# Gated scan of the second block: gate bias fetched a stage earlier, squares of the queries and keys on ScalarE, and another order of the steps' rows

## What is computed

```python
def _mlstm_scan(q, k, v, li, lf, state):      # chunks of 128 tokens
    def step(carry, inp):
        C, n, m = carry
        qc, kc, vc, lic, lfc = inp
        b = jnp.cumsum(lfc, axis=-1)
        logd = jnp.where(mask, b[..., :, None] - b[..., None, :] + lic[..., None, :], -jnp.inf)
        inter = b + m[..., None]
        m_s = jnp.maximum(inter, jnp.max(logd, axis=-1))
        dmat = jnp.exp(logd - m_s[..., None])
        s = jnp.einsum('bhsd,bhrd->bhsr', qc, kc) * dmat
        ...
        log_w = b[..., -1:] - b + lic
        m_new = jnp.maximum(b[..., -1] + m, jnp.max(log_w, axis=-1))
        w = jnp.exp(log_w - m_new[..., None])
        decay = jnp.exp(b[..., -1] + m - m_new)
        C_new = decay[..., None, None] * C + jnp.einsum('bhr,bhrv,bhrk->bhvk', w, vc, kc)
...
gates = z[..., 4 * M_W:G_END] + b_gates       # input and forget gates; lf = log_sigmoid(forget gate)
q_a = _rms_norm(z[..., a0:a0 + A_W].reshape(B_, L_, A_HEADS, A_DH), qn_w)
k_a = _rms_norm(z[..., a0 + A_W:a0 + A_W + A_KVW].reshape(B_, L_, A_KV, A_DH), kn_w)
```

## Time and profile before

| | us |
|---|---|
| median of 3 runs | 4027.12 |
| lowest, highest | 4027.06, 4028.39 |
| profiled execution, its own time | 4033.01 |
| profiled execution, span | 4031.2 |
| TensorE busy | 3406.1 (84%) |
| VectorE busy | 1940.7 (48%) |
| ScalarE busy | 677.4 (17%) |
| GpSimd busy | 941.4 (23%) |

### The profile page before, as it was taken

One profiled execution on the slowest core, in us unless ns is written; L12 is line 12 of the kernel. 1 busy time (PEld: TensorE's weight loads), 2 busy tenths in 40 slices (PEclk: granted clock), 3 DMA queues, 4 the chain that ended last, 5 costly groups with the idle time before them and its releaser, 6 DMA issues. The chain is left out here.

```text
span 4031.2 us, 37513 instructions
## 1 busy us (share of the span) xinstructions
PE 3406.1 (84%) x11902; PEld 1511.2 (37%) x11903; DVE 1940.7 (48%) x3995; ACT 677.4 (17%) x1600; POOL 941.4 (23%) x811
## 2 busy tenths in 40 slices
PE   7988999668899987999868967789878888788877
PEld 3345444422233322333225445444333333333332
DVE  5834222522233322333225236476666766677676
ACT  1011211000000000000002125312222222222221
POOL 2000000022122222021221040014444444444443
PEclk8999999789999999999989988789999899899998
DMA  9825423369998998296975100239999999999997
GB/s 332 281 105 177 168 101 133 125 242 408 371 384 346 365 407 347 96 389 262 383 305 183 53 7 1 84 125 408 421 421 409 421 410 412 421 405 421 416 421 317
DMA packets 194149, 1157.36 MB, mean 287 GB/s; under 512 B 25659, under 2 KB 27995, under 8 KB 74356
## 3 DMA queue, kind: packets, MB, share of 16 engines
q1 hardware_dynamic: 97140, 565.17, 36.2%
q0 software_dynamic: 80576, 564.05, 34.1%
q10 hardware_dynamic: 16320, 26.75, 2.1%
HBM read 1128.96 MB, written 48.68 MB: 292 GB/s over the span
## 5 line engine op out<-in xcount | busy, mean ns | idle before, releaser
L1149 PE MATMUL ps<-wt,e_xT 128*64 128x512 f32 x3200 | 741.1, 608 | 115.5 <-DMA wt<-in_w_exp 114.7
L2559 DVE SCALAR_TENSOR_TENSOR mod<-q_uv,mix 128x1024 f32<-128x1024 f32 x512 | 627.1, 1225 | 389.7 <-DMA q_uv<-in_peer_uv,q_picks 384.4
L2264 POOL DMA_INDIRECT q_uv<-in_peer_uv,q_picks x512 | 573.5, 1120 | 997.4 <-PE ps L2356 715.8
L2356 PE MATMUL ps<-q_uv,q_dg 128*128 128x512 f32 x1024 | 517.3, 662 | 136.8 <-ACT q_dg L2433 136.7
L2356 PE MATMUL ps<-q_uv,tri 128*128 128x512 f32 x1024 | 474.7, 618 | 80.8 <-ACT tri L2433 80.4
L1129 POOL COPY wt<-e_land 128x2048 f32<-128x2048 f32 x124 | 247.9, 2029 | 1002.7 <-PE ps L1149 951.1
L1149 PEld LDWEIGHTS ps<-wt,e_xT 128*64 128x64 f32 x3200 | 219.5, 139 | 595.5 <-issue 381.6
L2356 PEld LDWEIGHTS ps<-q_uv,q_dg 128*128 128x128 f32 x1024 | 212.2, 212 | 432.9 <-issue 432.9
L1149 PE MATMUL ps<-wt,e_aT 128*64 128x512 f32 x1600 | 354.8, 596 | 2.8 <-ACT e_aT L1202 2.8
L2356 PEld LDWEIGHTS ps<-q_uv,tri 128*128 128x128 f32 x1024 | 198.5, 198 | 353.4 <-issue 353.4
L454 PE MATMUL ps<-hT,wt 128*128 128x512 f32 x640 | 285.1, 602 | 1.5 <-DVE wt L781 1.5
(11 more groups left out here) (447 smaller groups left out, 3411.8 us busy)
## 6 DMA issues: line engine op xcount, KB each, us to landing
wt<-in_w_exp SPq DMA_DIRECT2D x260, 1024.0 KB, 19.3
e_land<-in_w_exp SPq DMA_DIRECT2D x124, 1024.0 KB, 24.1
wt<-in_w_in_units SPq DMA_DIRECT2D x15, 2048.0 KB, 11.3
mod<-in_w_mod_units SPq DMA_DIRECT2D x48, 512.0 KB, 5.6
scratch_xs<-const_zeros SPq DMA_DIRECT2D x8, 2080.0 KB
mod<-in_w_ada_units SPq DMA_DIRECT2D x32, 512.0 KB, 8.5
p_ring<-in_w_in SPq DMA_DIRECT2D x7, 2048.0 KB, 10.4
e_xg<-scratch_xs ACTq DMA_DIRECT2D x104, 128.0 KB, 6.9
```

The costliest lines, as they stand in the source:

```text
L1149: ins = nc.tensor.matmul(ps[64 * h:64 * h + 64, at, :], lhs[:, k % 4, 64 * (k // 4):64 * (k // 4) + 64], wt[:, u, a, h * W:(h + 1) * W], s ...
L2264: pool.indirect_dma_start(out=uv[:, n % NR, :, :].rearrange("p a d -> p (a d)"), out_offset=None, in_=A["peer_uv"], in_offset=bass.Indirec ...
L2356: last = nc.tensor.matmul(acc(t)[:, c, :], dg(n), uv[:, n % NR, 1, c * W:(c + 1) * W], start=fresh, stop=closing)
L2559: dve.scalar_tensor_tensor(junk[:, n % 2, :], uv[:, n % NR, 0, :], 1.0, mix[:, tile_of(k), :], ALU.mult, ALU.mult, accum_out=ap[:, k % 2, ...
```

## The change

There are three edits. The bias `bg` becomes a tensor that both stages share, and SyncE fetches it in `second_project`, behind the weights; that stage ends only when it has landed. The squares are made by ScalarE behind its Ln, no longer by GpSimd, and VectorE sums them behind `aa` instead of ahead of it. And TensorE's list has the rows of steps 0 to 3 ahead of `states(0)`, and those of steps 4 and 5 ahead of the wait for the state; VectorE's `state(1)` moves from the end of step 4 to behind the six steps.

```diff
@@ build: tensors of the second block
-                     zr=sb("zr", [P, NT + NTC, 784], c=second))
+                     zr=sb("zr", [P, NT + NTC, 784], c=second),
+                     bg=sb("bg", [P, 16], c=second))
@@ second_project, SyncE, behind the last weights(n)
+                sp.dma_start(S["bg"][:, :], A["b_gates_2"].unsqueeze(0).broadcast_to([P, 16])).then_inc(s_bg, 16)
                 sp.wait_ge(s_g2, 16)
+                sp.wait_ge(s_bg, 16)
@@ second_heads
-        bg = sb("bg", [P, 16])
+        bg = S["bg"]
@@ SyncE
-                sp.dma_start(bg[:, :], A["b_gates_2"].unsqueeze(0).broadcast_to([P, 16])).then_inc(s_bg, 16)
                 sp.dma_start(negm[:, :, :], K["negm"]).then_inc(s_load, 16)
@@ GpSimd
-                pool.tensor_tensor(sq[:, :, :], zr[:, :, 16:16 + 10 * DH], zr[:, :, 16:16 + 10 * DH], ALU.mult).then_inc(s_sq, 1)
                 pool.wait_ge(s_load, 16 * 5)
                 pool.wait_ge(s_rr, 1)
@@ TensorE
                 pe.wait_ge(s_aa, 1)
-                spreads(0)
-                spreads(1)
-                spreads(2)
+                for i in range(4):
+                    spreads(i)
                 states(0)
-                spreads(3)
+                spreads(4)
+                spreads(5)
                 pe.wait_ge(s_C, 1)
                 states(1)
-                spreads(4)
-                spreads(5)
                 pe.wait_ge(s_ar, NSTEP)
@@ ScalarE, behind Ln
+                act.activation(sq[:, :, :], zr[:, :, 16:16 + 10 * DH], ACT.Square).then_inc(s_sq, 1)
                 act.wait_ge(s_rq, 1)
                 act.activation(rq[:, :, :], rq[:, :, :], ACT.Sqrt).then_inc(s_sd, 1)
@@ VectorE
-                dve.wait_ge(s_bg, 16)
                 link(dve.tensor_tensor(gt[:, :, :], zr[:, :, 0:16], bg[:, :].unsqueeze(1).broadcast_to([P, NA, 16]), ALU.add))
@@
                 dve.tensor_tensor(lf[:, :, :, :], le[:, :, :, :], lf[:, :, :, :], ALU.subtract).then_inc(s_lf, 1)
-                dve.wait_ge(s_sq, 1)
-                link(dve.tensor_reduce(rq[:, :, :].rearrange("p t h -> p (t h)"),
-                                       sq[:, :, :].rearrange("p t (h c) -> p (t h) c", c=DH), AX_X, ALU.add))
-                dve.tensor_scalar(rq[:, :, :], rq[:, :, :], 1.0 / DH, RMS_EPS, ALU.mult, ALU.add).then_inc(s_rq, 1)
                 link(dve.memset(mr[:, 0, :], 0.0))
                 dve.wait_ge(s_cum, 1)
@@
                 last.then_inc(s_aa, 1)
                 dve.wait_ge(s_aa, 1)
+                dve.wait_ge(s_sq, 1)
+                link(dve.tensor_reduce(rq[:, :, :].rearrange("p t h -> p (t h)"),
+                                       sq[:, :, :].rearrange("p t (h c) -> p (t h) c", c=DH), AX_X, ALU.add))
+                dve.tensor_scalar(rq[:, :, :], rq[:, :, :], 1.0 / DH, RMS_EPS, ALU.mult, ALU.add).then_inc(s_rq, 1)
@@
                     if i == 3:
                         state(0)
-                    if i == 4:
-                        dve.wait_ge(s_xk, 1)
-                        state(1)
@@
                 dve.tensor_scalar(eq[:, 1], eq[:, 1], -1.0, None, ALU.mult).then_inc(s_eq, 1)
+                dve.wait_ge(s_xk, 1)
+                state(1)
                 dve.wait_ge(s_xq, 1)
```

More of the change, by code:

```diff
@@ L1347, in second_project @@
         s_h, s_ht, s_hT, s_full, s_free = sem("h"), sem("ht"), sem("hT"), sem("full"), sem("free")
+        s_bg = sem("bg")
         s_dve, s_zp, s_conv, s_ct, s_kt, s_kc = sem("dve"), sem("zp"), sem("conv"), sem("ct"), sem("kt"), sem("kc")
@@ L1656, in second_heads @@
         rd = sb("rd", [P, 2, AKV])
-        s_bg, s_load, s_dve, s_abs, s_lf1, s_one, s_lf2, s_lf = (sem(n) for n in ("bg", "load", "dve", "abs", "lf1", "one", "lf2", "lf"))
+        s_load, s_dve, s_abs, s_lf1, s_one, s_lf2, s_lf = (sem(n) for n in ("load", "dve", "abs", "lf1", "one", "lf2", "lf"))
         s_cum, s_aa, s_ab, s_ar, s_ek, s_xk, s_eq, s_xq, s_wsc = (sem(n) for n in (
```

## The result

| | before | changed |
|---|---|---|
| median, us | 4027.06 (5 runs) | 4002.71 (5 runs) |
| lowest to highest | 4017.74 to 4028.39 | 3992.35 to 4007.77 |
| span of the profiled execution | 4031.2 | 3990.6 |

The ratio is 0.9943, 95% interval 0.9925 to 0.9962: 23 us faster, between 15 and 30. A later set of runs of the same two kernels gave 0.9956 (0.9942 to 0.9969; medians 4023.37 and 4005.02). The forecast was 4005.8, 21.3 less than before.

The account below looks back on a forecast made before the run. second_heads up to the end of its scan was taken to bound, its saving moving the last stage forward whole. Start 8.7 plus steps 12.7 gave 21.3 us off: 4027.1 to 4005.8, range 4002 to 4012, chance 0.72.

Parts of the forecast that it names:

- Start: Beginning of second_heads up to step 0's reduction of the running maxima on VectorE, claimed to come 8.7 us earlier.
- Steps: Six steps of running maxima on VectorE: idle times of 3.80 and 6.81 and state(1)'s 2.07 go, 12.7 us.
- No idle time is left on VectorE: In the six steps: TensorE's reordered rows arrive in time, so VectorE no longer waits for them.
- the later overlap: GpSimd's query and key chain beside VectorE's scan: shared port costs single short VectorE operations some tenths each.
- `state(1)` behind the steps: Update moved behind step 5: hidden by decayed(0)'s wait for ScalarE, so no cost taken; 2.1 us without that cover.
- the 0.9 put down for half speed: First product with CT behind the steps: possible 0.9 us cost with TensorE at half speed, not taken into the sum.
- from E to the end the same length as before: From the first instruction behind step 5 to the end of second_heads: length unchanged, no gain.
- GpSimd's chain: Queries and keys on GpSimd in second_heads: ends 17 us before TensorE wants it, instead of 29.
- rivals, 1 and 2: At second_heads' start: gate sum slow by itself, 4009.2, chance 0.05; extra table load before Square, 4007.1, chance 0.1.
- Rival 3: TensorE stays at half clock in the six steps: 15.5 us off, 4011.6, chance 0.08.
- Rival 4: Half clock over the states' rounds behind the steps makes the kernel slower, up to 8 us, 4035; chance 0.02.
- Rival 5: GpSimd's chain or the wait for the squares replaces the removed idle time: no change, 4027, chance 0.03.

Follow-up runs that it names:

- e1_bias: Kernel before with the bias alone fetched in second_project; from ScalarE's first table load in second_heads to step 0's reduction 19.37 us, before 19.62.
- e2_squares: Kernel before with squares on ScalarE and their reduction behind aa, nothing else; from ScalarE's first table load to step 0's reduction 12.92 us, before 19.62.
- e7_reduce_first: Changed kernel with the reduction of the squares put back ahead of the copies of TensorE's sums; stage start to step 0's reduction 16.42 us, changed kernel 10.78.
- e4_memset: Kernel before with GpSimd's squares replaced by a memset of the same tile; stage start to step 0's reduction 15.87 us, before 19.62.
- e3_order: Kernel before with only the order of TensorE's rows and the place of state(1) changed; whole time ratio 0.9972 (0.9961 to 0.9984).
- e11_delay: Changed kernel with two unused ScalarE copies ahead of the attention's first scores; TensorE's first query transpose to stage end 142.1 us, changed kernel 137.6 and 137.3.
- e9_early: Changed kernel with the gates' whole chain and the squares with their sums moved into second_project; 4004.65 us (0.9948 of the kernel before).
- e12_early_fill: e9_early with unused TensorE products ahead of each attention pair's scores, 22 for pairs 3 to 11, else 6; 4015.54 us (0.9976 of the kernel before).
- e13_less_fill: e12_early_fill with fewer unused products, 10 for pairs 3 to 11, else 2; 3996.88 us against 4023.44 for the kernel before (0.9935).

## Why the prediction was right

The direction, the size and the chain of reasons held. Term by term:

- **Start, 8.7 forecast, 8.84 measured.** The transfer's 2.7 and the hold of 3.85 go, and ScalarE's table becomes the next late thing, as worked out (Exp at S + 1.29). Gate sum 0.26 (0.25 forecast), Square 3.39 (3.45), reduction beside the rows of step 0. e1_bias and e2_squares show that neither of the first two gives this alone, and e7_reduce_first that the move of the reduction carries 5.6 of it. That GpSimd's instruction was the holder is shown by e4_memset, and by e1_bias, where the hold passed to the next instructions.
- **Steps, 12.7 forecast, 11.0 measured** (E - T 34.04 before, 23.03 after). Two terms of the sum were mis-sized. "No idle time is left on VectorE" was off by 0.85: TensorE's granted clock stayed at half (1.2 GHz) for longer behind the start of the rows than in the profile before, so the rows of step 1 came late. It was 0.50 to 0.52 in their first 6 us, against 0.53 in the first 4 and 1.00 after (windows below). And in step 4 VectorE's addition (L2012) was held 1.04 by GpSimd's operation of 1.26 (L1724), which starts 0.07 ahead of it and ends with it: the later overlap that I had put at some tenths.
- **`state(1)` behind the steps, nothing forecast.** The update ends at E + 3.79 and the first product with `CT` at E + 5.9, and ScalarE takes it at E + 6.59 without having waited for it (line below), so it cost nothing. E to Q is 43.99 against 44.86, and that 0.87 less need not be the change's: e4_memset, with the order of before, has 43.7, and the last product of the rounds (L1801) ran in 2.06 instead of 3.35. Also the 0.9 put down for half speed did not come: in e3_order and e7_reduce_first the product with `CT` took 3.8, and E to Q was 43.8 and 43.6.
- **Attention, nothing forecast, 2.6 to 3.2 gained.** It is the one part that I did not see, against "from E to the end the same length as before" (181.6 instead of 185.1, 3.5 less). S to Q fell by 20.7 only, and this gain made 23.4 of it for the stage. What sets this length stays open: the experiments rule out the attention's code, its start alone and its mean clock, and e11_delay shows that a delay ahead of it moves it.
- **The range.** 4002.71 lies 0.7 above its lower bound, and there luck has a part. The range gave 1.3 to the scatter of whole times, by three runs; the five runs of each kernel span 10.7 and 15.4 us, and the interval of the ratio stands for 15 to 30 us. What the runs bear out is the working inside the stage; the whole time alone could not have told 21.3 from 24.
- GpSimd's chain ended at S + 62.8, 15 us ahead of TensorE's wait (17 forecast).

The windows over the rows of the first steps, in the kernel before and in the changed one (the last number but two is the granted clock):

```profile
2372.45:2376.45 4.00, 4.00 (x19) 4.00 (x20) 0.00 (x0) 0.05 (x1) 0.00 (x0) 0.53 0.01 4
2376.45:2380.45 4.00, 3.64 (x31) 3.29 (x29) 3.49 (x9) 0.08 (x1) 0.00 (x0) 1.00 0.01 2
```

```profile
2354.26:2358.26 4.00, 4.00 (x18) 4.00 (x19) 4.00 (x1) 1.19 (x1) 0.00 (x0) 0.50 0.02 6
2358.26:2360.26 2.00, 2.00 (x11) 2.00 (x11) 1.80 (x5) 1.53 (x2) 0.00 (x0) 0.52 0.00 0
2360.26:2364.26 4.00, 4.00 (x38) 4.00 (x37) 3.15 (x7) 1.26 (x5) 0.73 (x1) 1.00 0.00 0
```

ScalarE's timeline of the changed kernel, where it takes the first product with `CT` (no idle time in brackets):

```profile
2385.83 2.43 ACT L1874 ACTIVATE h_qT<-ko,h_ek 128x128 f32<-128x128 f32 x8
2388.17 2.13 ACT L1905 ACTIVATE h_num<-ps,h_wsc 128x129 f32<-128x129 f32 x8
```

Of the rivals, 1 and 2 were refuted by the trace (gate sum 0.26, no load before Square). Rival 3 came true for the rows of step 1 alone (0.85 of its 5.8). Rival 4's half clock over the rounds was not seen: the granted clock from E to Q was 0.93, 0.89 before. Rival 5's wait did not come.

What stays open beside the attention's length: where each microsecond of the whole time's 24.3 that is not in `second_heads` lies, since over all profiles P scatters by 10 us and the last stage by 8.

## What to carry to other kernels

When a short instruction takes microseconds, look whose instruction on the engine beside it ends at the same moment; then taking away the wait in front of it gives nothing (0.25 us here) until that work moves to another engine (then it gives 2.1). For an in-order list, put long work of no urgency behind the signal that lets the next engine start, and put everything that needs only a free buffer ahead of what waits for a value. Price a change inside a stage by lengths within the stage, and do not trust a gain behind it that no edit explains.

## What the runs showed of the hardware

- Two VectorE `tensor_scalar` with one input in SBUF were held 6.3 us by a GpSimd `tensor_tensor` (e1_bias), and 0.2 by a memset (e4_memset); the `tensor_tensor` just before them, with two inputs in SBUF, was held 3.85 by the GpSimd `tensor_tensor` (kernel before) and not by the memset. The Trainium skill ("SBUF — State Buffer", Who interferes with whom) has the rule that fits both: a `tensor_scalar` in its two-port mode takes the shared pair, while a `tensor_tensor` meets only GpSimd's reads. That the `tensor_scalar` ran in that mode no run shows.
- Which of the two started first decided who was held: with 0.08 us of lead the gate sum was free (e1_bias), and 0.07 behind GpSimd's operation the addition L2012 was held 1.04 (changed kernel).
- For the same rows TensorE's granted clock was 0.53 in the first 4 us and 1.00 in the next 4 in the kernel before, and 0.50 to 0.52 in the first 6 in the changed one. In e9_early, where the projections end 1.59 us ahead of the rows, it was 1.00 from their start (64 products in 7.38 us instead of 10.21).
- One unused product of 128 by 128 in 32-bit floats took 0.235 us at full clock (e12_early_fill; 0.25 in e13_less_fill), and with ten of them in 2.86 us of idle time the granted clock stayed at 1.00.
- A higher mean granted clock did not go with a shorter attention as a whole: 0.83 and 0.88 for 137.6 and 137.3 us (changed kernel), 0.83 and 0.89 for 142.7 and 142.6 (e9_early, e13_less_fill).
